# Two factor operations moved ahead of a level of the inverse, and a constant matmul halved

## What is computed

```
def step(S, inp):
    r_t, w_t, k_t, v_t, a_t, b_t = inp
    sa = jnp.einsum('bhij,bhj->bhi', S, a_t)
    S = (S * w_t[:, :, None, :] + sa[..., None] * b_t[:, :, None, :]
         + v_t[..., None] * k_t[:, :, None, :])
    y_t = jnp.einsum('bhij,bhj->bhi', S, r_t)
    return S, y_t
...
kk = k * k_k.reshape(A_HEADS, A_HEAD_DIM).astype(jnp.float32)
kk = kk / jnp.maximum(jnp.sqrt(jnp.sum(kk * kk, axis=-1, keepdims=True)), 1e-12)
k = k * (1.0 + (a - 1.0) * k_a.reshape(A_HEADS, A_HEAD_DIM).astype(jnp.float32))
decay = jnp.exp(-jnp.exp(w))
y = _wkv7_scan(r, decay, k, v, -kk, kk * a)
y = _layer_norm(y, lnx_g.reshape(A_HEADS, A_HEAD_DIM), lnx_b.reshape(A_HEADS, A_HEAD_DIM), GN_EPS)
y = y + jnp.sum(r * k * r_k.astype(jnp.float32), axis=-1, keepdims=True) * v
```

## Time and profile before

| | us |
|---|---|
| median of 3 runs (2843.96 to 2846.32) | 2846.18 |
| the profiled execution | 2847.68 |
| its span, first to last instruction | 2845.6 |
| PE busy, of the span | 2688.5 (94%) |
| DVE busy | 1267.5 (45%) |
| ACT busy | 516.4 (18%) |
| POOL busy | 585.6 (21%) |

### The profile page before, as it was taken

The page is one execution under the profiler, slowest core; times in us unless marked ns, Lnnn a source line. Parts: engine busy times, 40 slices in busy tenths (PEclk is TensorE's granted clock), DMA queues, the critical chain, the costliest instruction groups (busy, mean ns, idle before and its releaser), DMA issues. The chain is left out here.

```text
span 2845.6 us, 46016 instructions
## 1 busy us (share of the span) xinstructions
PE 2688.5 (94%) x20310; PEld 2018.3 (71%) x20310; DVE 1267.5 (45%) x1973; ACT 516.4 (18%) x1028; POOL 585.6 (21%) x328
## 2 busy tenths in 40 slices
PE   6999989989999999999888899999999999999998
PEld 4656567764888887444666648888878764788886
DVE  1221233442899954203667645452232373544333
ACT  3222122221111101112444311000010062100001
POOL 0000055520000000000222104333333100344431
PEclk9999999999999999999999999999999999999999
DMA  6223100002222123111000012222222200122220
GB/s 286 79 108 139 60 2 2 2 24 105 80 89 89 63 82 122 59 73 61 3 3 3 3 39 81 89 89 89 89 77 103 89 1 30 69 83 86 89 89 30
DMA packets 17222, 196.33 MB, mean 69 GB/s; under 512 B 1880, under 2 KB 2008, under 8 KB 5248
## 3 DMA queue, kind: packets, MB, share of 16 engines
q1 hardware_dynamic: 17024, 193.39, 17.8%
HBM read 191.27 MB, written 2.12 MB: 68 GB/s over the span
## 5 line engine op out<-in xcount | busy, mean ns | idle before, releaser
L3140 PE MATMUL psum<-arena,weight_ring 128*128 128x256 f32 x3072 | 670.9, 379 | 2.4 <-ACT arena L3030 2.4
L3140 PEld LDWEIGHTS psum<-arena,weight_ring 128*128 128x128 f32 x3072 | 582.8, 190 | 85.0 <-ACT arena L3030 4.6
L1788 PE MATMUL psum<-arena,weight_ring 128*128 128x256 f32 x1584 | 348.2, 381 | 5.0 <-DVE arena L1964 4.0
L1788 PEld LDWEIGHTS psum<-arena,weight_ring 128*128 128x128 f32 x1584 | 301.6, 191 | 48.7 <-issue 6.4
L2300 POOL TENSOR_TENSOR arena<-arena,consts_sb 128x512 f32<-128x512 f32 x48 | 64.6, 1352 | 919.4 <-ACT arena L2626 719.0
L473 PE MATMUL psum<-arena,weight_ring 128*128 128x512 f32 (+1 forms) x672 | 248.1, 529 | 2.7 <-ACT arena L606 2.7
L473 PEld LDWEIGHTS psum<-arena,weight_ring 128*128 128x128 f32 x672 | 127.9, 192 | 114.9 <-issue 106.2
L226 PE MATMUL psum<-arena,weight_ring 128*128 128x512 f32 x384 | 168.8, 602 | 0.0
L3239 POOL TENSOR_TENSOR weight_ring<-arena,weight_ring 128x1024 f32<-128x1024 f32 x32 | 79.3, 2479 | 378.9 <-PE psum L3140 378.9
L226 PEld LDWEIGHTS psum<-arena,weight_ring 128*128 128x128 f32 x384 | 74.1, 193 | 92.9 <-issue 92.9
L3229 POOL TENSOR_TENSOR arena<-weight_ring 128x1024 f32<-128x1024 f32 x32 | 76.9, 2404 | 305.2 <-POOLq L2923 275.7
(11 more groups left out here) (467 smaller groups left out, 3750.1 us busy)
## 6 DMA issues: line engine op xcount, KB each, us to landing
weight_ring<-in_mlp_up SPq DMA_DIRECT2D x16, 2048.0 KB, 7.7
weight_ring<-in_mlp_down SPq DMA_DIRECT2D x16, 2048.0 KB, 7.7
weight_ring<-in_ada SPq DMA_DIRECT2D x12, 2048.0 KB, 12.6
weight_ring<-in_gate_up SPq DMA_DIRECT2D x11, 2048.0 KB, 7.7
weight_ring<-in_w_in SPq DMA_DIRECT2D x7, 2048.0 KB, 10.9
weight_ring<-in_w_o SPq DMA_DIRECT2D x4, 2048.0 KB, 7.9
weight_ring<-in_w_kv SPq DMA_DIRECT2D x4, 2048.0 KB, 7.9
weight_ring<-in_down_a SPq DMA_DIRECT2D x4, 1536.0 KB, 6.4
```

The costliest lines, as they stand in the source:

```text
L1788: mm = pe.matmul(g.banks[i][:, pair * half:(pair + 1) * half], left[:, j, pair * P:(pair + 1) * P], right(j), start=first and j == 0, stop ...
L3140: mm = pe.matmul(g.banks[i][:, pair * HALF:(pair + 1) * HALF], left[:, j, pair * P:(pair + 1) * P], right(j), start=first and j == 0, stop ...
```

## The change

On VectorE `scaled` is cut in two. Its first operation (L2763, `at_` times `ep`, with its two waits) becomes `scaled_first`. `bonus_terms(a)` and `scaled_first(a)` are now called ahead of `level(b, 2)`; the rest of `scaled` stays behind it. On TensorE the constant matmul ahead of `raw_b(a)` has 256 columns in place of 512 in trips 1 to 7; the condition `on(b)` that goes was always true there, so no call is added or taken away. In trip 0 nothing changes.

```diff
                     if on(a):
-                        for _ in range(6 if a == 0 else 1 if on(b) else 0):
-                            keep_busy(pe, g, g.banks[4], SEQ)
+                        for _ in range(6 if a == 0 else 1):
+                            keep_busy(pe, g, g.banks[4], SEQ if a == 0 else 256)
                         raw_b(a)
...
-                def scaled(p):
+                def scaled_first(p):
                     dve.wait_ge(s.agkk, p + 1)
                     dve.wait_ge(s.exp, 4 * p + 1)
                     dve.tensor_tensor(at_, at_, ep, ALU.mult).then_inc(s.prep, 1)
+
+                def scaled(p):
                     dve.wait_ge(s.exp, 4 * p + 3)
...
+                    if on(a):
+                        bonus_terms(a)
+                        scaled_first(a)
                     if on(b):
                         level(b, 2)
                     if on(a):
-                        bonus_terms(a)
                         scaled(a)
```

## The result

| | before | changed |
|---|---|---|
| median of four runs | 2846.25 us | 2824.81 us (2822.66 to 2827.13) |
| profiled execution, its span | 2845.6 us | 2820.7 us |

The ratio is 0.9925, with an interval of 0.9908 to 0.9942: 21 us faster (16.5 to 26.2 by the interval), where 16.7 was forecast.

What follows compares the result with a forecast made beforehand. TensorE was busy for 94% of the span; its largest reachable wait was the raw product's for the last factor, 13.0 us. From 2846.2, 12.9 for waits and 3.8 for clock gave 2829.5 us, range 2824 to 2839.

Steps and rivals of the forecast that it cites:

- Ahead of level 2: VectorE, before level 2's subtraction: two moved operations, 1.23 us together, fill idle time; cost 0, at most 0.1 a trip.
- The cover: VectorE's spare time between the moved operations' end (1539.76) and level 2's subtraction (1539.93): 0.17 us.
- Behind level 2: VectorE after level 2's transpose: last factor ends before meeting GpSimd's mask, so the raw product starts 2.31 us earlier.
- The part of the meeting: VectorE's factor standing while GpSimd's mask runs: avoiding it gives 1.08 of the raw product's 2.31 us.
- The constants: TensorE before the raw product: 256 columns end near 1543.0, covered by the last factor; by itself worth nothing.
- What is late next: TensorE's L2481 waits for L2725, caught by the mask: 0.64 us lost, 1.67 a trip left in trips 3 to 7.
- The clock: TensorE's stretches at the lower granted clock: 3.8 us gained together, bounds 0 and 7.3.
- trip 3's stretch: Long lower-clock stretch of TensorE after the raw product's wait in trip 3: 2.7 us, counted as gained.
- the four others: Shorter lower-clock stretches late in trips 4 to 7, 1.15 us each, behind a wait for L2782; one counted as gone.
- the 7.3: Upper bound in us for TensorE's clock gain, if all the lower-clock stretches counted in trips 3 to 7 go.
- The rival of the constants: Halved constants let TensorE's clock fall at the raw product in all seven trips: 19.7 us more, 2853; chance 0.05.

Runs made afterwards that it cites:

- the first comparison: The changed kernel (two factor operations moved, 256-column constants) run beside the kernel before: 2824.81 us, ratio 0.9925.
- in the second: The changed kernel, unaltered, run once more against the kernel before: 2826.01 us, ratio 0.9927.

## Why the prediction was right, and where not

**Ahead of level 2: right.** The cover was 0.17 us deep by the sum, and level 2 waits 0.17 us in the trace.

**Behind level 2: right.** The last factor begins 1.89 us behind the transpose's start (1.92 in the sum) and the mask 0.21 behind that (0.18). The part of the meeting is shown by itself: with the wait on GpSimd the raw product's own wait is 1.07 us shorter (1.08 in the sum), of which the trip keeps 0.3, from 36.26 to 35.96, since the unit norm is caught. Moving one operation gives 35.60. Moving both gives 34.46. The first operation is worth 0.66 and the second 1.14, since only with both does the last factor come ahead of the mask.

**The constants: right.** Nothing by themselves, nothing when left wide, nothing when taken out, to within what the medians can tell; the trips bear it out, but for 0.5 and 0.4 us in trips 1 and 2.

**What is late next: right, 0.13 small.** L2725 was caught and L2481 waits 0.52 us for it (0.64 in the sum). The trip is 36.26 - 34.46 = 1.80 us shorter in place of 1.67. For trips 1 and 2, trip 0-1 went from 27.56 to 25.21 and trip 1-2 from 32.05 to 29.71, so 2.35 and 2.34 (2.30 and 2.23 in the sum). The waits come to 5 x 1.80 + 2.35 + 2.34 = 13.7 us, for 12.9.

**The clock: the term that was mis-sized.** I had counted trip 3's stretch at 2.7 and one of the four others, 3.8 in all, because the wait for L2782 that goes before them stays. It did not bring them back: the wait is still there, 0.78 us in the changed kernel, and three of its four trips between the marks of trips 3 and 7 run through it at the full clock. In the profiled executions the stretches of before cost 3.0 + 1.4 + 1.2 + 1.5 in the trips by the marks, about 1.3 more behind the mark in trip 7 (an estimate, the mean of the others), and 3 for the long one; the one of after cost 1.5. That is 9.9, and with 13.7 it makes 23.6, as against the stage's 333.63 - 310.26 = 23.4. (The spans of the two profiles differ by 24.9; where the other 1.5 us went, outside the stage, was not looked into.) Over medians it was less: the changed kernel was 21.4 us faster in the first comparison and 20.2 in the second, which leaves 7.7 and 6.5 for the clock; the two profiles of the changed kernel show how the stretches differ between executions. I left the long stretch behind trip 8 out of the sum altogether, though it was in the trace. So the 7.3 that I took for all stretches was no upper bound, and with it goes a slip: the sum with 7.3 gives 2826.0, where I wrote 2825. That the total fell within 5 us of the forecast owes something to luck, as the clock's term moves by as much from one execution to the next.

**The rival of the constants** fell. Of its claim one thing stands: constants put into the waits of 1.9 and 0.78 us kept the clock up in trips 3 to 7 of the kernel before. At the raw product they need not be there once that wait is gone.

## What to carry to other kernels

Ask of a late operation not only what stands ahead of it, but which other engine it meets: moving two operations of 0.6 us moved the last factor by 2.3, because it came to lie ahead of a mask. The meeting is not removed, it is handed to the next in line, so look for who can bear it. And a trip has to be compared at one clock: here the change took away 13.7 us of waits and brought 6.5 to 9.9 more from the clock, and two executions of one program differed by 4.5 us in it.

## What the runs showed of the hardware that I had not expected

An operation over 7 columns, 0.15 us alone, took 1.23 when it met a GpSimd operation, 1.08 more; one over 512 columns paid 1.07. So what was paid hung on how long the other still ran, not on its own length. A wait added on GpSimd alone, in the right place, made the kernel 0.38% faster (interval 0.23 to 0.53), and in the place of the mask before it 0.20% slower. Adding 1024 columns of useless constants to each trip, inside waits, gave 0.23% (0.12 to 0.33), with the stretches of trips 3 to 7, which cost 1.2 to 3.0 us each, gone.
